# Block attention inside a fused two-block network: how the probabilities are turned, and when the second group's scores and softmax run

## What is computed

```
qa = rmsnorm(heads(aq), q_norm_gain);  ka = rmsnorm(heads(ak), k_norm_gain);  va = heads(av)
rel_own = qpos[:, None] - offs[None, :]
lg_own  = einsum('bhqd,bhkd->bhqk', qa, ka) * scale + bias_table[:, t5_bucket(rel_own)]
probs   = softmax(where(rel_own >= 0, lg_own, NEG_INF))
out     = einsum('bhqk,bhkd->bhqd', probs, va)
```

## Time and profile before

| what | us |
|---|---|
| median of 3 runs (805.80 to 806.04) | 805.86 |
| the profiled execution | 806.31 |
| its span, first to last instruction | 804.5 |
| PE busy in the span | 797.9 |
| DVE busy | 597.5 |
| ACT busy | 540.0 |
| POOL busy | 132.8 |

### The profile page before, as it was taken

The page is one execution under the profiler, slowest core; times in us unless marked ns, Lnnn a source line. Parts: engine busy times, 40 slices in busy tenths (PEclk is TensorE's granted clock), DMA queues, the critical chain, the costliest instruction groups (busy, mean ns, idle before and its releaser), DMA issues.

```text
span 804.5 us, 11934 instructions
## 1 busy us (share of the span) xinstructions
PE 797.9 (99%) x4440; PEld 691.2 (86%) x4440; DVE 597.5 (74%) x837; ACT 540.0 (67%) x882; POOL 132.8 (17%) x232
## 2 busy tenths in 40 slices
PE   8999999999999999999999999999999999999998
PEld 8999788888888999887888888888989899888887
DVE  6999877666556579987776666556867689998764
ACT  6897578667756567656877677737664857677442
POOL 2040035344402000000244444202100000000000
PEclk9999999999999999999999999999999999999999
DMA  8955788765665564436676666665564463553511
GB/s 274 340 172 156 233 240 278 212 196 187 202 198 173 158 204 143 152 103 179 210 242 206 190 187 202 190 198 188 163 192 134 142 198 124 176 173 126 184 67 53
DMA packets 118972, 147.74 MB, mean 184 GB/s; under 512 B 7283, under 2 KB 89987, under 8 KB 118787
## 3 DMA queue, kind: packets, MB, share of 16 engines
q1 hardware_dynamic: 117539, 145.32, 57.2%
q10 hardware_dynamic: 1376, 1.66, 0.7%
HBM read 145.89 MB, written 2.63 MB: 185 GB/s over the span
## 4 chain that ended last, share of the span: by engine, by line
PE 96%; ACT 2%; DVE 1%; issue 0%; ACTq 0%
PE bank L573 22%; PE bank L575 21%; PE bank L574 21%; PE bank L498 6%; PE bank L499 6%; PE bank L500 6%; PE bank L538 3%; PE bank L540 1%; PE bank L505 1%; PE bank L506 1%; PE bank L507 1%; PE bank L938 1%; PE bank L600 1%; ACT whi L1156 1%; PE bank L816 1%; PE bank L799 1%
## 5 line engine op out<-in xcount | busy, mean ns | idle before, releaser
L1753 DVE TENSOR_TENSOR wlo<-raw,whi 128x1024 fp32r<-128x1024 f32 (+1 forms) x268 | 320.1, 1235 | 53.0 <-ACT whi L1156 52.4
L1156 ACT ACTIVATE whi<-raw 128x1024 fp32r<-128x1024 f32 (+1 forms) x260 | 258.7, 1046 | 78.7 <-PE bank L575 55.5
L573 PE MATMUL bank<-whi,xboth 128*128 128x512 f32 x464 | 182.0, 392 | 0.7 <-DVE xboth L1794 0.3
L575 PE MATMUL bank<-whi,xboth 128*128 128x512 f32 x464 | 180.6, 389 | 0.0
L574 PE MATMUL bank<-wlo,xboth 128*128 128x512 f32 x464 | 180.6, 389 | 0.0
L1130 POOL COPY xg<-sq 32x128 f32<-32x128 f32 x176 | 97.6, 555 | 132.7 <-DVE sq L2110 126.3
L573 PEld LDWEIGHTS bank<-whi,xboth 128*128 128x128 f32 x464 | 87.1, 188 | 20.2 <-issue 2.0
L575 PEld LDWEIGHTS bank<-whi,xboth 128*128 128x128 f32 x464 | 87.1, 188 | 18.1
L574 PEld LDWEIGHTS bank<-wlo,xboth 128*128 128x128 f32 x464 | 87.2, 188 | 17.7
L498 PE MATMUL bank<-xboth,whi 128*128 128x256 f32 x352 | 100.6, 286 | 0.8 <-DVE xboth L1794 0.8
L499 PE MATMUL bank<-xboth,whi 128*128 128x256 f32 x352 | 99.6, 283 | 0.0
(11 more groups left out here) (364 smaller groups left out, 1267.0 us busy)
## 6 DMA issues: line engine op xcount, KB each, us to landing
raw<-in_ffn_w_in SPq DMA_DIRECT2D x176, 256.0 KB, 3.6
raw<-in_w_in SPq DMA_DIRECT2D x48, 512.0 KB, 4.4
raw<-in_ffn_w_out SPq DMA_DIRECT2D x44, 512.0 KB, 4.2
raw<-in_attn_w_qkv SPq DMA_DIRECT2D x24, 512.0 KB, 4.6
raw<-in_lru_w_in SPq DMA_DIRECT2D x14, 512.0 KB, 7.6
raw<-in_lru_w_out SPq DMA_DIRECT2D x8, 512.0 KB, 3.7
raw<-in_attn_w_o SPq DMA_DIRECT2D x8, 512.0 KB, 5.0
raw<-in_w_out SPq DMA_DIRECT2D x8, 512.0 KB, 4.3
```

The source lines that it names most:

```text
L573: nc.tensor.matmul(dst, hi, wh, start=start, stop=False)
L575: return nc.tensor.matmul(dst, lo, wh, start=False, stop=stop)
L1156: nc.scalar.activation(whi[:, c % RING, part], raw[:, c % RAWS, part], ACT.Copy).then_inc(hi_done, 1)
L1753: nc.vector.tensor_tensor(wlo[:, c % RING, part], raw[:, c % RAWS, part], whi[:, c % RING, part].bitcast(F32), ALU.subtract).then_inc(lo_d ...
```

## The change

Six things are done. The line numbers in the order listings of "after" are those of the changed file.

- `moba_transposes` and `moba_copies` are gone. At the end of `moba_scale(g)`, DVE waits for its own eight multiplications and turns all of `pp_` (128x1536) in 32x32 blocks into a new tile `p_blocks[g]`.
- POOL carries three of the four 32-partition strips to `pt`: 12 copies of 32x384 for each group. ACT carries the fourth: 4 copies of 32x384 (`moba_moves`).
- `moba_values(g)` waits for these (`p_pool`, `p_act`), and for the maxima of group 1, since it overwrites bank 4.
- `moba_scores(1)` moves from after chunk 10 to after chunk 8; it waits for the maxima of group 0. `moba_values(0)` moves from after chunk 9 to after chunk 10. `moba_values(1)` stays after chunk 13.
- On DVE `decay_start` moves ahead of `moba_scale(0)`, `moba_max(1)` from c = 11 to c = 9, `moba_scale(1)` from c = 12 to c = 10, `moba_out(0)` from c = 10 to c = 11. On ACT `moba_exp(1)` moves from after the split at c = 11 to before the split at c = 10.
- `p_blocks[0]` lies on `kb` and `cum`, so ACT's sigmoid into `kb` and DVE's `decay_sum` wait for the strips of group 0.
- Each head's 384 columns are stored in another order (the 128 columns of the first query block first). Counts and sizes of matmuls are the same.

```diff
-                    pe.wait_ge(mpv_read, g)
+                    pe.wait_ge(nm_ready, g)
...
-            def moba_transposes(g):
-                for n in range(4):
-                    pe.wait_ge(p_ready, 4 * g + n + 1)
-                    for d0, s0 in ((0, S), (P, 0), (S, P)):
-                        last = nc.tensor.transpose(bank[4 + n][:, d0:d0 + P], pp_[:, n, s0:s0 + P], ident)
-                    last.then_inc(pt_mm, 1)
...
+                pe.wait_ge(p_pool, g + 1)
+                pe.wait_ge(p_act, g + 1)
+                pe.wait_ge(nm_ready, 2)
...
-                8: [lambda: moba_transposes(0)],
-                9: [lambda: moba_values(0)],
-                10: [lambda: moba_scores(1)],
-                12: [lambda: moba_transposes(1)],
+                8: [lambda: moba_scores(1)],
+                10: [lambda: moba_values(0)],
                 13: [lambda: moba_values(1)],
...
+            for g in range(2):
+                pool.wait_ge(p_turned, g + 1)
+                if g:
+                    pool.wait_ge(mpv_mm, g)
+                    pool.wait_ge(p_pool, g)
+                for i in range(3):
+                    for j in range(4):
+                        dst = pt[32 * j:32 * j + 32].rearrange("p h (d n) -> p (h d) n", n=P)
+                        last = nc.gpsimd.tensor_copy(dst[:, :, 32 * i:32 * i + 32],
+                                                     p_blocks[g][32 * i:32 * i + 32, :, j, :])
+                last.then_inc(p_pool, 1)
...
-            def moba_copies(g):
+            def moba_moves(g):
+                act.wait_ge(p_turned, g + 1)
+                if g:
+                    act.wait_ge(mpv_mm, g)
+                for j in range(4):
+                    dst = pt[32 * j:32 * j + 32].rearrange("p h (d n) -> p (h d) n", n=P)
+                    last = nc.scalar.activation(dst[:, :, 96:128], p_blocks[g][96:128, :, j, :], ACT.Copy)
+                last.then_inc(p_act, 1)
...
+                dve.wait_ge(p_ready, 4 * g + 4)
+                nc.vector.transpose(p_blocks[g][:, :, :, :].rearrange("p e f n -> p (e f) n"),
+                                    whole(pp_).rearrange("p (b n) -> p b n", n=32)).then_inc(p_turned, 1)
```

More of the change, by code:

```diff
@@ L257, in build @@
         pt = over("probs_t", 40, [P, 4, 384])
+        p_blocks = [over(f"p_blocks{n}", kb, [P, 12, 4, 32]) for n, kb in enumerate((8, 54))]
         ag = over("ag", 46, [P, 2, PAIR])
@@ L337, in build @@
             sem, ("msq", "msq_hi", "msq_lo", "mss", "msd", "mn_ready", "mean_in"))
-        sc_mm, sc_read, nm_ready, p_exp, p_ready, pt_mm, pt_read, mpv_mm, mpv_read = map(
-            sem, ("sc_mm", "sc_read", "nm_ready", "p_exp", "p_ready", "pt_mm", "pt_read",
+        sc_mm, nm_ready, p_exp, p_ready, p_turned, p_pool, p_act, mpv_mm, mpv_read = map(
+            sem, ("sc_mm", "nm_ready", "p_exp", "p_ready", "p_turned", "p_pool", "p_act",
                   "mpv_mm", "mpv_read"))
@@ L887, in moba_scores @@
                     q, k = mq[r0:r0 + 64, f, :], mk[r0:r0 + 64, f, :]
-                    nc.tensor.matmul(bank[4 + n][:, 0:S], q[:, P:S], k, start=True, stop=True)
-                    nc.tensor.matmul(bank[4 + n][:, S:384], q[:, 0:P], k[:, 0:P], start=True, stop=True)\
+                    nc.tensor.matmul(bank[4 + n][:, P:384], q[:, P:S], k, start=True, stop=True)
+                    nc.tensor.matmul(bank[4 + n][:, 0:P], q[:, 0:P], k[:, 0:P], start=True, stop=True)\
                         .then_inc(sc_mm, 1)
-            def moba_transposes(g):
-                for n in range(4):
-                    pe.wait_ge(p_ready, 4 * g + n + 1)
-                    for d0, s0 in ((0, S), (P, 0), (S, P)):
-                        last = nc.tensor.transpose(bank[4 + n][:, d0:d0 + P], pp_[:, n, s0:s0 + P], ident)
-                    last.then_inc(pt_mm, 1)
-            def moba_values(g):
-                for n in range(4):
-                    pe.wait_ge(pt_read, 4 * g + n + 1)
+            def moba_values(g):
+                pe.wait_ge(p_pool, g + 1)
+                pe.wait_ge(p_act, g + 1)
+                pe.wait_ge(nm_ready, 2)
+                if g:
+                    pe.wait_ge(mpv_read, g)
                 pe.wait_ge(banks_read, b0 + 6 + 4)
@@ L1592, in moba_exp @@
                 for n in range(4):
-                    for m, (s0, s1) in enumerate(((0, S), (S, 384))):
+                    for m, (s0, s1) in enumerate(((P, 384), (0, P))):
                         col = 2 * n + m
@@ L1636, in _ @@
                 if c == 9:
-                    moba_copies(0)
+                    moba_moves(0)
+                if c == 10:
+                    moba_exp(1)
+                if c == 11:
+                    moba_moves(1)
                 if c == 4:
@@ L1653, in _ @@
                 if c == 10:
+                    act.wait_ge(p_pool, 1)
+                    act.wait_ge(p_act, 1)
                     nc.scalar.activation(whole(kb), whole(fb), ACT.Sigmoid, scale=-1.0).then_inc(k_sig, 1)
@@ L1657, in _ @@
                     nc.scalar.preload_act_table_set("natural_log_exp_and_others")
[L1658 to L1661, removed]
                 if c >= 14 and c - 13 < len(LEVELS):
@@ L2334, in moba_max @@
                 dve.wait_ge(bias_in, 16)
+                if g:
+                    dve.wait_ge(p_turned, g)
                 for n in range(4):
                     dve.wait_ge(sc_mm, 4 * g + n + 1)
-                    for m, (s0, s1, o0) in enumerate(((0, S, 0), (S, 384, P))):
+                    for m, (s0, s1, o0) in enumerate(((P, 384, 0), (0, P, P))):
                         k = 2 * n + m
@@ L2462, in _ @@
                 if c == 8:
+                    read(b0 + 7)
+                    decay_start()
                     moba_scale(0)
+                if c == 9:
+                    moba_max(1)
+                if c == 10:
+                    moba_scale(1)
                 if c == 11:
-                    moba_max(1)
-                if c == 12:
-                    moba_scale(1)
+                    moba_out(0)
                 if c == 4:
                     head_square_lo(1)
-                if c == 10:
-                    moba_out(0)
                 ahead(c0 + c)
@@ L2482, in _ @@
                     moba_max(0)
-                if c == 8:
-                    read(b0 + 7)
-                    decay_start()
                 if c == 10:
+                    dve.wait_ge(p_pool, 1)
+                    dve.wait_ge(p_act, 1)
                     decay_sum()
```

1 line of the change is left out of this document (added).

## The result

| what | before | after |
|---|---|---|
| median, us | 805.85 (14 runs, 805.78 to 806.10) | 807.51 (14 runs, 805.85 to 807.80) |
| ratio of the compared runs, 95% interval | 1 | 1.0015 (1.0008 to 1.0022) |
| the profiled execution, its span | 806.31, 804.5 | 807.43, 805.6 |

The change takes 24 transposes from PE and gains nothing. The times of after lie in two bunches: ten executions took 807.36 to 807.80 at a mean granted clock of 0.998, four took 805.85 to 806.04 at 0.999 or 1.0. The middle of the second bunch is 0.15 us above before, that of the first 1.8 us. Both need an explanation: where the 2.62 us of PE went, and what adds another 1.6 us in ten of fourteen executions. The median of 807.51 says only that more than half of the executions fell into the slower bunch.

A forecast was written before the change was run, and what follows sets the result against it. PE, busy 99%, was taken to bound the kernel; its 2.62 us gain is lost because DVE's keys, at 661.3 plus 2.4 for POOL, start `level(0)` at 663.8, +0.6: 805.86 + 0.6 = 806.5 us, range 804.0 to 808.3.

The forecast's parts named there:

- its own mechanism: Around `level(0)`: the gain on PE is eaten by DVE, -0.2 to +1.5 us, chance 0.46.
- PE loses 2.62 us: On PE: two sets of 12 transposes at 1.31 us each go, gaining 2.62 us if PE never waits.
- Rival (d): On PE: the transposes hide behind other PE work, so the change does not relieve PE; chance 0.01.
- ACT's chain: ACT from 617.74: gapless work through splits, strip copies and `decay_ln`; group 1's exponentials run from 629.37 to 632.90.
- DVE up to the split of c = 10: DVE after group 1's exponentials: starts at 633.03, multiplications 2.08, turn 1.77, split of c = 10 at 636.95.
- What POOL adds: DVE beside POOL's group 1 copies: blocked splits, element-wise operations and running sums are late by 2.3 us, taken as 2.4.
- rival (b): DVE beside POOL's copies: only element-wise operations block, not running sums; -0.6 us, 805.3, chance 0.18.
- rival (c): POOL's strip copies over `decay_sum`: slower than the line says; with 0.75 us each, +2.5 us, 808.4; chance 0.19.
- `level(0)` 0.6 later than before: Start of `level(0)`: keys ready at 663.7, so it starts at 663.8 against 663.20, +0.6 us.
- Rival (a): DVE beside POOL's copies: they cost DVE little; -1.8 or -2.6 us, time 803.2 to 804.1, chance 0.16.
- Group 0's copies cost nothing, and group 1's are hidden from PE: POOL: group 0's copies end near 632, 2.5 us to spare; group 1's near 650, before the values at about 653.
- "Behind `level(0)` the three engines stand to one another as before": After `level(0)`: DVE's 1.85 us of idle time are used up, and nothing is gained back.

The follow-up runs named there:

- the last experiment: Changed kernel with keys ahead of the split at c = 14, `moba_out(0)` behind that of c = 11, ACT carrying group 1's strips in two portions: 803.46 us.
- one copy: Changed kernel with only one of POOL's 12 strip copies of group 1, the other eleven left out: 804.73 us, ratio 0.998.
- keys first: Changed kernel with group 1's result copy and the turned keys ahead of DVE's split of the next chunk at c = 14: 804.15 us, ratio 0.9974.
- one more evacuation moved: Changed kernel with the turned keys ahead of the split at c = 14, and `moba_out(0)` behind the split of c = 11: 804.08 us, ratio 0.9974.
- filler: Changed kernel with 12 useless transposes of the identity put where PE waits before `level(0)`: 806.22 us, ratio 1.0.
- the turn without the new order: Changed kernel with turn and POOL's and ACT's strips, but group 1's scores and softmax and group 0's values placed as before: 816.22 us, ratio 1.0122.

## Why the prediction was right, and where it was not

The range of 804.0 to 808.3 around the forecast of 806.5 us holds the measured 807.51, but not for its own reason alone: +1.7 us is just outside the -0.2 to +1.5 that the prediction gave its own mechanism, and above the 807.5 from which it spoke of slower. Step by step:

- **PE loses 2.62 us: right.** The last experiment gets exactly this, 2.63, where nothing waits. Rival (d), hidden transposes, is out.
- **ACT's chain: right.** First exponential of group 1 at 628.85 + 0.50 = 629.35 (predicted 629.37), and ACT is through with them at 632.37 + 0.50 = 632.87 (632.90). Strip copies 0.52 each, 2.12 for four with 0.54 from start to start in between (2.16).
- **DVE up to the split of c = 10: right.** Reciprocal at 633.00 (633.03), the turn 1.78 (1.77), the split at 636.90 (636.95). From there to the keys 26.2 us, of which 1.9 are POOL's: 24.3 undisturbed, predicted 24.4.
- **What POOL adds: right in kind, 0.5 us too large.** Against the undisturbed rows of the last experiment: second half of the split of c = 10, 0.31 (0.31); the two operations of `decay_sum`, 0.08 and 0.18 (0.15 and 0.22); four running sums 0.96 (1.15); the split of c = 11, 0.36 (0.47). Sum 1.9, predicted 2.3 and taken as 2.4. The running sums do block and are blocked, as the Trainium skill (SBUF — State Buffer, "Who interferes with whom") says of an instruction with two SBUF inputs; the trace now agrees, with 918 ns beside a copy and 666 without. So rival (b), only element-wise operations, is out, and rival (c) too: a copy takes 0.50, as the line through the earlier trace rows gave.
- **`level(0)` 0.6 later than before: it was 0.04 earlier.** The misses are 0.5 from POOL's sum, 0.1 from DVE's path and the start of PE. The place and the cause were right: PE waits for `turn_keys`, 1.8 us (predicted 2.2), and at chunk 13 it loses 0.62 us (predicted 1), 0.36 of which shows as a wait. Rival (a) would have been right about the direction of this miss, but the copies are far from free.
- **Group 0's copies cost nothing, and group 1's are hidden from PE: right.** They end at 632.1 and 650.1 on before's axis (632 and 650 predicted), and no wait for `p_pool` shows on PE.
- **"Behind `level(0)` the three engines stand to one another as before": this step failed.** In the profiled execution PE ran at half its clock for 3.4 us right behind the wait, and `level(1)` came 1.66 us late. I had costed a PE wait at its length and looked at PE's clock only to see that it was full before. The sum was 0.6 with no clock in it; measured were 0.15 without the fall and 1.8 with it. No row of before has a wait of PE in this stage, so none showed this price. In hindsight the right forecast has two values, before + 0.2 or before + 1.6 to 1.8, each with a fair chance (15 of 25 executions took the second).

That the median lies within 1 us of the forecast is thus partly luck: one term was 0.6 too high, a term of 1.7 was missing, and the median goes with how many executions the clock fell in (807.51 in the first set, 806.51 in the second).

## What to carry to other kernels

Work that leaves the bounding engine is worth its time only if what that engine does next is ready earlier too: look up, for each operation behind the removed one, which engine brings its input and by how much it was early. Here one exchange on DVE turned a loss of 0.15% into a gain of 0.26%, without a change in the work. A wait of PE may cost more than its length: here a change that traded 2.62 us of work for waits of about the same length lost 1.4 to 1.7 us on top in 15 of 25 executions, and filling the wait with useless work brought no loss in 11. Where two engines block one another, move the copies to a third engine, in portions that leave its own deadlines alone; cutting them alone brought less here (ratio 0.9996).

## What the runs showed of the hardware

- **TensorE's clock after a wait.** After a wait of 1.8 us before `level(0)` the granted clock fell to half in 15 of 25 executions; after one of 3.1 us in 7 of 11; with waits of 0 to 0.8 us there in none of 43 (one copy, keys first, one more evacuation moved, filler, two portions). The lengths of the waits are those of the one profiled execution of each kernel. With 1.8 us at `moba_values(1)` instead, two of 11 executions show 0.998 and lie 1.3 and 1.6 us above the rest's median of 805.59. After the 4.7 and 3.8 us in the turn without the new order, four of four have 0.994. A fall behind the wait of 1.8 us lasted 3.4 us in both traces that show one; it cost 1.7 us in the trace of after, and the two bunches are 1.4 to 1.6 us apart. What decides whether a wait of 1.8 us brings one is not settled here.
- **POOL and DVE take turns.** A split behind a copy of 32x384 is late by 0.31 us and behind one of 32x192 by about 0.15; a running sum is late by 0.25 and 0.09. A blocked copy grows from 0.50 to up to 1.47 us, with the length of the operation before it. The DVE operations that read a bank keep their length (0.69 us for `moba_out` in the middle of POOL's copies and without them). Two tiles as inputs are not needed for it: `decay_keys`, which multiplies one tile in place in SBUF, takes 0.43 us in the median of its four beside copies of 192 columns and 0.35 without.
- **A running sum of 128x256 counts among the blocked ones**: 0.67 us alone, 0.92 beside copies of 384 columns, 0.76 beside copies of 192.
